# Delta-rule stage of a hybrid block: pairs of chunks overlapped on alternating banks, outputs alternating halves

## The reference, cut to what matters

```python
def gdn_chunked(q, k, v, log_a, beta, s0):
    ...
    g = jnp.cumsum(log_a.reshape(B, H, n, C), axis=-1)
    decay = jnp.where(incl, jnp.exp(jnp.where(incl, diff, 0.0)), 0.0)
    kb = k * beta
    a_mat = jnp.where(strict, jnp.einsum('bhnid,bhnjd->bhnij', kb, k) * decay, 0.0) + jnp.eye(C)
    rhs = jnp.concatenate([v * beta, kb * jnp.exp(g)[..., None]], axis=-1)
    sol = lax.linalg.triangular_solve(a_mat, rhs, left_side=True, lower=True)
    u, w = sol[..., :DV], sol[..., DV:]
    qk = jnp.einsum('bhnid,bhnjd->bhnij', q, k) * decay
    ...
    def step(s, xs):
        v_new = u_c - w_c @ s                 # einsums, per head
        o = qd_c @ s + qk_c @ v_new
        s = s * ge_c + ke_c.T @ v_new
```

## Time and profile before

| | |
|---|---|
| profiled execution | 2245.06 us, span 2243.3 us, mean granted clock 0.935 |
| TensorE busy | 2012.8 us (90%) |
| VectorE busy | 1165.2 us (52%) |
| ScalarE busy | 992.2 us (44%) |
| GpSimd busy | 141.7 us (6%) |
| DMA | 254.61 MB, mean 114 GB/s |
| the delta-rule stage | from 1066.11 (first sums) to 1302.98 (last output copy) |

### The profile page before, as it was taken

How to read it: one execution, slowest core, us unless ns; L and a number is a source line. 1 busy time by engine, 2 the same in 40 slices (tenths; PEclk the granted TensorE clock), 3 DMA queues, 4 the chain that set the end, 5 groups by cost and what they waited for, 6 DMA issues and landing times.

```text
span 2243.3 us, 41597 instructions
## 1 busy us (share of the span) xinstructions
PE 2012.8 (90%) x16886; PEld 1763.1 (79%) x16886; DVE 1165.2 (52%) x1785; ACT 992.2 (44%) x1590; POOL 141.7 (6%) x132
## 2 busy tenths in 40 slices
PE   5998899979999999899788879998778998798997
PEld 4783687867878778688677869997677998677997
DVE  4421678734533442554455447645556655676654
ACT  5333477523431332445322246544745545455543
POOL 0000100001000001000323210010010000010000
PEclk8999899859999999999899979999989999999999
DMA  8330377512233323333100035663334665404663
GB/s 265 87 118 19 112 209 238 157 38 75 85 94 94 94 87 93 86 85 113 31 4 4 2 89 159 182 185 112 103 104 135 185 177 169 113 21 140 185 179 115
DMA packets 441804, 254.61 MB, mean 114 GB/s; under 512 B 10816, under 2 KB 440512, under 8 KB 441536
## 3 DMA queue, kind: packets, MB, share of 16 engines
q1 hardware_dynamic: 441664, 252.59, 38.9%
HBM read 251.51 MB, written 1.05 MB: 113 GB/s over the span
## 4 chain that ended last, share of the span: by engine, by line
PE 81%; DVE 10%; ACT 5%; issue 2%; DMA 1%; POOL 0%; DVEq 0%; ACTq 0%; SPq 0%; POOLq 0%
PE bank L378 20%; PE bank L380 19%; PE bank L379 19%; PE bank L370 3%; PE bank L603 2%; PE bank L604 2%; PE bank L1876 2%; DVE weights_lo L328 2%; ACT weights_hi L321 2%; PE bank L941 1%; PE bank L1168 1%; PE bank L1978 1%; PE bank L611 1%; PE bank L1892 1%; PE bank L475 1%
## 5 line engine op out<-in xcount | busy, mean ns | idle before, releaser
L328 DVE TENSOR_TENSOR weights_lo<-ring,weights_hi 128x1024 fp32r<-128x1024 f32 x472 | 578.2, 1230 | 471.4 <-ACT weights_hi L321 467.6
L378 PE MATMUL bank<-x_hi,weights_hi 128*128 128x256 f32 (+1 forms) x2024 | 644.1, 318 | 82.4 <-DVE x_lo L406 29.4
L321 ACT ACTIVATE weights_hi<-ring 128x1024 fp32r<-128x1024 f32 x472 | 495.1, 1054 | 352.4 <-PE bank L380 317.7
L380 PE MATMUL bank<-x_hi,weights_lo 128*128 128x256 f32 (+1 forms) x2024 | 636.8, 315 | 0.0
L379 PE MATMUL bank<-x_lo,weights_hi 128*128 128x256 f32 (+1 forms) x2024 | 636.7, 315 | 0.0
L378 PEld LDWEIGHTS bank<-x_hi,weights_hi 128*128 128x128 f32 x2024 | 389.5, 192 | 115.0 <-issue 87.8
L379 PEld LDWEIGHTS bank<-x_lo,weights_hi 128*128 128x128 f32 x2024 | 389.0, 192 | 24.5 <-issue 1.2
L380 PEld LDWEIGHTS bank<-x_hi,weights_lo 128*128 128x128 f32 x2024 | 389.3, 192 | 23.9
L378 PE MATMUL bank<-hidden_hi,weights_hi 128*128 128x256 f32 (+1 forms) x864 | 270.7, 313 | 10.0 <-DVE hidden_lo L1442 6.8
L380 PE MATMUL bank<-hidden_hi,weights_lo 128*128 128x256 f32 (+1 forms) x864 | 271.9, 315 | 0.0
L379 PE MATMUL bank<-hidden_lo,weights_hi 128*128 128x256 f32 (+1 forms) x864 | 271.6, 314 | 0.0
(11 more groups left out here) (316 smaller groups left out, 2449.8 us busy)
## 6 DMA issues: line engine op xcount, KB each, us to landing
ring<-mlp_w SPq DMA_DIRECT2D x128, 512.0 KB, 4.0
ring<-ada_w SPq DMA_DIRECT2D x96, 512.0 KB, 4.7
ring<-w_ffn_in SPq DMA_DIRECT2D x88, 512.0 KB, 4.7
ring<-w_ffn_out SPq DMA_DIRECT2D x32, 512.0 KB, 3.7
ring<-gdn_w_in SPq DMA_DIRECT2D x24, 512.0 KB, 3.9
ring<-even_w_in SPq DMA_DIRECT2D x18, 512.0 KB, 4.9
ring<-w_out SPq DMA_DIRECT2D x16, 512.0 KB, 5.2
ring<-w_in_a SPq DMA_DIRECT2D x14, 512.0 KB, 3.8
```

What stands on the lines that cost most here:

```text
L321: nc.scalar.activation(w_hi[:, g % AHEAD, :], ring[:, g % RAW, :], ACT.Copy).then_inc(hi_done[g % AHEAD].sem, 1)
L328: nc.vector.tensor_tensor(w_lo[:, g % AHEAD, :], ring[:, g % RAW, :], w_hi[:, g % AHEAD, :].bitcast(F32), ALU.subtract).then_inc(lo_done[g ...
L378: pe.matmul(dst, lhs[0](k), rhs[0](k), start=start and k == 0, stop=False)
L380: last = pe.matmul(dst, lhs[1](k), rhs[0](k), start=False, stop=stop and k == nk - 1)
```

## The change

- Pairs use banks by turns: pair `p`, unit `z` has `bank[4z + 2(p % 2)]` and the next one for everything: levels, values, weights and steps. The separate `bank_r` is gone.
- `DE`, `NA`, `XT` and `XX` exist twice. The second set lies in the memory of `weights_lo`. So the low parts of the four first output tiles are no longer made in `dve_odd_in`, but one by one in the last part of the stage. For pair 3 the last state, decayed queries, `QKT` and `U` lie in memory of earlier buffers.
- The head of pair `p + 1` is taken apart and placed among the levels of pair `p` on every engine. The values of pair `p` come after the matrix start of `p + 1`; its weights stand in level 0 of `p + 1`.
- For the latent pairs, the query sums and query-key products stand in the levels of pair 3.
- The outputs of both latent pairs are accumulated in the same four banks, so VectorE copies each once. Products with the states alternate between the two halves of rows and so between two banks. They are placed between the steps of pair 3.
- The norm's first squares wait for the first two output copies instead of all. SyncE's load of the next tables waits for the same last copy, counted anew.

```diff
+        with nc.sbuf_tensor("spare", [P, AHEAD * TILE], F32) as spare:
+            pass
         w_lo = sb("weights_lo", [P, AHEAD, TILE], F32R)
...
+        DE1, NA1, XT1, XX1 = (by_heads(spare[:, i * UNIT:(i + 1) * UNIT], C) for i in range(4))
+        DE, NA, XT, XX = (DE0, DE1), (NA0, NA1), (XT0, XT1), (XX0, XX1)
...
             for i in range(VB):
-                split_lo(dve, odd_tiles.first + NB_CONV + i + AHEAD)
+                if i + AHEAD < VB:
+                    split_lo(dve, odd_tiles.first + NB_CONV + i + AHEAD)
...
-        def bank_a(z):
-            return bank[4 * z]
...
+        def bank_of(p, z, i):
+            return bank[4 * z + 2 * (p % 2) + i]
...
         def pe_gdn_ws(pe, p, st):
...
+                pe.wait_ge(N["wtc"], u + 1)
+                if st == 1 and p < 2:
+                    pe.wait_ge(N["d"], 2 * (p + 2) + z + 1)
+                if st == 1 and p == 2:
+                    pe.wait_ge(N["qe"], z + 1)
...
+        def obank(b):
+            return bank[(0, 1, 4, 5)[b]]
+        def pe_gdn_o_values(pe, p, h2):
+            pe.wait_ge(N["vn"], 4 * (p + 1))
+            pe.wait_ge(N["qkt"], 4)
+            for par in range(2):
+                b = 2 * h2 + par
+                for i in range(2):
+                    hd = 2 * (2 * h2 + i) + par
+                    for z in range(2):
+                        at = (2 * i + TBS[p][z]) * P
+                        ins = pe.matmul(obank(b)[:, at:at + P], U[p][:, z, hd, :], QKT[p][:, z, hd, :], ...)
+        def pe_gdn_o_states(pe, p, h2):
+            pe.wait_ge(N["ss"], 2 * p + 8)
+            pe.wait_ge(N["qd"], 2 * (p - 1))
+            for i in range(2):
+                hp = 2 * h2 + i
+                for z in range(2):
+                    for st in range(2):
+                        c = st if z == 0 else 1 - st
+                        at = (2 * i + TBS[p][z]) * P + c * C
+                        for par in range(2):
+                            pe.matmul(obank(2 * h2 + par)[:, at:at + C], state(2 * p + st, z, hp, half(par)),
+                                      qdcs[p][half(par), z, hp, c * C:(c + 1) * C], ...)
         def pe_gdn(pe):
...
+            for p in range(4):
+                pe_gdn_q(pe, p, 0)
+                if p >= 1:
+                    pe_gdn_weights(pe, p - 1)
+                pe_gdn_z(pe, p, 0)
+                for st in range(2):
+                    pe_gdn_q(pe, p, 1 + st)
+                    if p >= 1:
+                        pe_gdn_ws(pe, p - 1, st)
+                    pe_gdn_z(pe, p, 1 + st)
+                    if p >= 1:
+                        pe_gdn_su(pe, p - 1, st)
+                    if p == 3:
+                        pe_gdn_query_sums(pe, 2 + st)
+                    elif st == 0:
+                        pe_gdn_sums(pe, p + 1)
+                pe_gdn_q(pe, p, 3)
+                if p < 3:
+                    pe_gdn_keys(pe, p + 1)
+                else:
+                    pe_gdn_query_keys(pe, 2)
+                    pe_gdn_query_keys(pe, 3)
+                pe_gdn_z(pe, p, 3)
+                pe_gdn_q(pe, p, 4)
+                pe_gdn_z(pe, p, 4)
+                if p < 3:
+                    pe_gdn_first(pe, p + 1)
+                pe_gdn_values(pe, p)
+            pe_gdn_weights(pe, 3)
             pe_gdn_ws(pe, 3, 0)
+            pe_gdn_o_values(pe, 2, 0)
+            pe_gdn_o_states(pe, 2, 0)
             pe_gdn_su(pe, 3, 0)
+            pe_gdn_o_values(pe, 2, 1)
             pe_gdn_ws(pe, 3, 1)
-            pe_gdn_o(pe, 3)
+            pe_gdn_o_states(pe, 2, 1)
+            for h2 in range(2):
+                pe_gdn_o_states(pe, 3, h2)
+            for h2 in range(2):
+                pe_gdn_o_values(pe, 3, h2)
...
         def act_gdn(act):
+            act_gdn_eyes(act, 0)
+            act_gdn_decay(act, 0)
             for p in range(4):
+                if p >= 1:
+                    act_gdn_values(act, p - 1)
+                act_gdn_level(act, p, 0)
+                if p >= 1:
+                    act_gdn_weights(act, p - 1)
+                act_gdn_level(act, p, 1)
+                if p == 3:
+                    act_gdn_query(act, 2)
+                act_gdn_level(act, p, 2)
+                if p == 3:
+                    act_gdn_query(act, 3)
+                else:
+                    act_gdn_decay(act, p + 1)
+                act_gdn_level(act, p, 3)
+                if p < 3:
+                    act_gdn_eyes(act, p + 1)
+                act_gdn_level(act, p, 4)
...
         def dve_gdn(dve):
...
+            for p in range(4):
+                dve_gdn_level(dve, p, 0)
+                for st in range(2):
+                    if p >= 1:
+                        dve_gdn_vn(dve, p - 1, st)
+                    dve_gdn_level(dve, p, 1 + st)
+                    if p >= 1:
+                        dve_gdn_ss(dve, p - 1, st)
+                    if p < 3 and st == 0:
+                        dve_gdn_decays(dve, p + 1)
+                dve_gdn_level(dve, p, 3)
+                if p < 3:
+                    dve_gdn_below(dve, p + 1)
+                else:
+                    dve_gdn_query(dve, 2)
+                dve_gdn_level(dve, p, 4)
+                if p < 3:
+                    dve_gdn_first(dve, p + 1)
+            dve_gdn_query(dve, 3)
             dve_gdn_vn(dve, 3, 0)
+            out_tiles = odd_tiles.first + NB_CONV + VB
+            dve.wait_ge(N["wt"], 8)
+            split_lo(dve, out_tiles)
             dve_gdn_ss(dve, 3, 0)
+            split_lo(dve, out_tiles + 1)
             dve_gdn_vn(dve, 3, 1)
+            split_lo(dve, out_tiles + 2)
+            for b in range(4):
+                dve_gdn_out(dve, b)
+            split_lo(dve, out_tiles + 3)
...
         def pool_gdn(pool):
...
+            for p in range(4):
+                if p >= 1:
+                    pool_gdn_scale_keys(pool, p - 1)
+                    pool_gdn_sg(pool, p - 1, 1)
+                if p < 3:
+                    pool_gdn_below(pool, p + 1)
+                if p == 2:
+                    pool_gdn_query_masks(pool, 2)
+                if p == 3:
+                    pool.wait_ge(N["wt"], 6)
+                    nc.gpsimd.memset(QKT[3], 0.0).then_inc(N["clear"], 1)
+                    pool_gdn_query_masks(pool, 3)
+                    pool_gdn_scale_queries(pool, 2)
+                if p < 2:
+                    pool_gdn_masks(pool, p + 2)
+                if p >= 1:
+                    pool_gdn_sg(pool, p, 0)
+            pool_gdn_scale_queries(pool, 3)
+            pool_gdn_scale_keys(pool, 3)
...
         def act_odd_out(act):
-            act.wait_ge(N["oc"], 8)
             for i in range(4):
+                act.wait_ge(N["oc"], 2 * (i // 2) + 2)
                 nc.scalar.activation(as_heads(obuf(osq, i)), two_heads(i), ACT.Square).then_inc(OT["squares"], 1)
```

More of the change, by code:

```diff
@@ L1497, in state @@
         def state(i, z, hp, rows=slice(0, P)):
+            if i == 7:
+                return last_state[rows, z, hp, :]
             if i % 3 == 0:
@@ L1908, in pe_gdn_tail @@
                     for c in range(2):
-                        ins = pe.matmul(four((bank_a(z), bank_b(z))[c])[half(hd % 2), hd // 2, :],
-                                        ktk[half(c), TBS[p][z], hd * C:(hd + 1) * C], XX[half(c), z, hd, :], start=True, stop=True)
+                        ins = pe.matmul(four(bank_of(p, z, c))[half(hd % 2), hd // 2, :],
+                                        ktk[half(c), TBS[p][z], hd * C:(hd + 1) * C], XX[p % 2][half(c), z, hd, :],
+                                        start=True, stop=True)
@@ L1930, in pe_gdn_ws, with pe_gdn_query_sums @@
+        def pe_gdn_query_sums(pe, p):
+            for z, u in units(p):
+                for hd in range(NH):
+                    col = la[:, TBS[p][z], z * NH + hd:z * NH + hd + 1].broadcast_to((P, C))
+                    ins = pe.matmul(bank_of(2, z, 1)[half(hd % 2), (hd // 2) * P:(hd // 2 + 1) * P], col, upto[:, z, :],
+                                    start=True, stop=True)
+                ins.then_inc(N["g2"], 1)
         def pe_gdn_ws(pe, p, st):
@@ L1969, in pe_gdn_o @@
                     for z in range(2):
-                        pe.matmul(o[:, (2 * i + z) * P:(2 * i + z + 1) * P], U[:, z, hd, :], QKT[:, z, hd, :],
-                                  start=i == 0 and z == 0, stop=False, skip_group_check=True)
-                for i in range(2):
-                    hp = 2 * h2 + i
-                    for z in range(2):
-                        for st in range(2):
-                            c = st if z == 0 else 1 - st
-                            at = (2 * i + z) * P + c * C
-                            ins = pe.matmul(o[:, at:at + C], state(2 * p + st, z, hp, half(par)),
-                                            qdc[half(par), z, hp, c * C:(c + 1) * C], start=False,
-                                            stop=i == 1 and z == 1 and st == 1, skip_group_check=True)
@@ new lines, in pe_gdn_o_values @@
```

(11 more changed lines are left out.)

309 lines of the change are left out of this document (125 added, 184 removed).

## The result

The changed kernel takes 2191.42 us (median of four runs, 2189.05 to 2191.99). The kernel before took 2239.28 us beside it (2239.13 to 2245.18), and the ratio is 0.977 with a 95% interval of 0.975 to 0.979. So 47.9 us went. The forecast was 47.6 us, to 2191.6. One execution of a later kernel, the one with eight unused products, took 3271.61 us at a mean granted clock of 0.551; it stands in none of the medians here.

The account below looks back on a forecast made before the run. TensorE was taken as the bound, 81% of the chain of waits. Gains of 32.2 (pairs), 13.1 (tail) and 3.5 (norm), less 1.2, gave 47.6 us: from the 2239.18 median to 2191.6, range 2177 to 2215.

Parts of the forecast that it names:

- fourth pair: Last pair of the delta-rule stage: output products leave, query work enters; 36.4 us work plus 5.0 gaps, 41.4 for 45.4.
- tail: After the fourth pair's values, to the last output copy: covered steps and state products at 0.12 us, 24.9 for 38.0.
- norm: Norm after the outputs: half the squares start 1.4 us sooner, four sums at full clock save 2.1; gain 3.5 us.
- moved splits: Four low parts of weights moved into the stage's tail, 1.23 us each on VectorE; one charged, 1.2 us lost.
- The heads: Serial sums, keys and inversion start before each pair: waits, 3.29 us and earlier engines' steps, fall beside TensorE work.
- The pauses: First pair's levels: 5.2 us of "issue", TensorE waiting for nothing the profile shows; no reordering removes it, so it stays.
- rival (a): TensorE's issue pauses vanish as slower pieces between levels let issue catch up: up to 18.2 us more, 2173; 7%.
- Rival (b): VectorE's fixed order becomes the bound, copies queue behind subtraction and head work: three pairs lose 5 us each, 2207; 20%.
- rival (c): Half clock stays in the tail: output matmuls take up to twice as long, norm's sums 2.1 us more, 2207; 13%.
- Rival (d): Alternating row halves in the tail's state products overlaps nothing: 7.7 us more, 2199; 10%.
- Rival (e): Slower: half clock spreads from the tail backward through the second to fourth pair, costing 108 us, 2300; 3%.
- Marks: Signs expected in the changed profile: level 0 start times, values' end, last copy, TensorE gaps, tail clock, and wrong-if limits.

## Why the prediction was right

The steps, in the two profiled executions:

| step | forecast gain | measured |
|---|---|---|
| first pair, 43.8 to 34.6 | 9.2 | 10.8 (33.0) |
| second pair, 45.6 to 39.2 | 6.4 | 7.6 (38.0) |
| third pair, 53.2 to 40.6 | 12.6 | 14.0 (39.2) |
| fourth pair, 45.4 to 41.4 | 4.0 | 1.6 (43.8) |
| tail, 38.0 to 24.9 | 13.1 | 15.1 (22.9) |
| norm | 3.5 | 3.7 |
| moved splits | -1.2 | not seen |
| sum | 47.6 | 52.8 |

The sum of the traces is 5 us more than that of the medians, 47.9. The profiled execution of before was 5.8 us above its median, and the stage of after was at the short end of its scatter. So the table as a whole is a little large, though which terms of it is not known, and the agreement of the totals to 0.3 us is partly luck: two executions of one kernel differ by 2.3 us in the stage alone, and the terms miss by up to 2.4 us each.

**The heads.** The mechanism was right. What my working lacked is that the head also costs the clock. I took TensorE's work and the wait and let the windows' clock of 0.94 pass into the start's 3.0 us; the run with serial heads shows 22.5 us for three of them, 13.6 of idle time and 8.9 of slower products. The sum came out right as I took TensorE's work at full clock and set it against windows of before that had the half clock in them.

**The pauses.** 5.2 us of "issue" in the first pair were kept in the forecast, and rival (a) gave them up. They stayed: in the chain of waits over the fourth pair they are still 13.1%.

```profile
by line: PE bank L1900 16.7%; issue 13.1%; PE bank L1917 11.0%; PE bank L1926 9.1%; PE bank L1957 8.7%; PE bank L1914 8.3%; DVE a L2184 7.4%; PE bank L1986 7.3%; PE bank L1974 6.3%; PE bank L1949 4.9%; PE bank L1936 2.3%; DVE spare L2166 1.
```

**The fourth pair** is the term that was off. I forecast 5.0 us of gaps, with the work at 36.4; busy time is 36.5, and the gaps are 7.3. 13.1% of 43.8 us are 5.7 us of pauses, which I had not counted here as such, and 7.4% is VectorE's query multiplication ahead of the copies, 3.2 us of the chain:

```profile
1222.92 3.48 DVE L2184 TENSOR_TENSOR a<-bank,arena 64x256 f32<-64x256 f32 x8
1226.43 0.72 DVE L2166 COPY_PREDICATED spare<-tables,bank 128x512 f32<-128x512 int32 x1
```

I had named this place and given it, with the empty cover behind level 4, 1.0 us. The values' wait is 2.26. Rival (b), VectorE's order as the bound, is true at this one place and nowhere else: it costs 2 us, not 15.

**The tail.** 0.12 us for a state product was taken between 0.09 and 0.24; it is 0.11. The 8.7 us for value products are 7.9 (2.05, 2.05 and 3.84). The clock was the open point. I gave rival (c) 13% and argued against it with TensorE's waiting ahead of the output products, and with the same products at the whole clock at 1248. Both facts hold, but neither settles the tail: without the alternation the clock fell with TensorE busy without a break. My forecast of 1.00 had no working for what the order of the halves does to the clock, and in that it was luck; it held since the change also alternates them. Had the alternation been left out, the stage would have been 14 us longer, near the 15.1 of (c), though half of it is the products themselves.

**Rival (d)**, alternation overlaps nothing, is out by the 0.11. **Rival (e)** is out: every window shows 1.00, and in the executions where the clock did fall within the pairs it came back.

**Marks.** Level 0 of pairs two to four was forecast near 1112, 1151 and 1192, and stands at 1110.4, 1148.4 and 1187.6; values end at 1231.4 for 1233, the last copy at 1254.3 for 1258. "No gap over 1.5 us" does not quite hold: TensorE pauses 1.64 us at 1220.92, inside a level's second half, and waits 2.26 us for the values. "Wrong if a pair takes over 44 us" was a near thing: the fourth took 43.8 in this execution and 45.3 in the second profile of the same kernel. TensorE does not stand idle for a weight tile ahead of the output projection: its wait there is 8.05 us for VectorE's `x_lo`, and was 8.06 before.

**How the 50 us of the stage divide.** Put back one at a time in the kernel after, serial heads cost 23.8 us, one-sided products 12.7 at their own place (14.2 over the stage), outputs behind the steps 2.5 (6.0). These are 39 to 44 of 50. Each is measured from the 186.9 us; from the second profile's 189.2 each stage figure is 2.3 less. The rest was not isolated; the whole-bank output copies and the moved query work are in it.

## What to carry to other kernels

Where TensorE is the bound and each block of work begins with a chain over four engines, put the next block's head into this block's body: it gave back the wait (13.6 us here) and also the half-clock stretch behind it (8.9). Where products use 64 rows of the weights, let the upper and lower half take turns, with a bank each; here it halved the time of each product and kept the clock, and the changed loops alone gave 0.8% of the whole program. Once few gaps are left, look for pauses at a fixed number of records: here they went with the instruction's number and not with what stood there. Fewer instructions would be the thing to try; no run tried it.

## What the runs showed of the hardware that was not expected

- Full activity does not keep the clock. In three executions of two kernels it was at 0.52, 0.54 and 0.67 over stretches of 21 to 22 us with TensorE busy 93 to 100% of them, where state products (64 rows, 128 columns) came from one half of the rows at a time; with the halves alternating it held 1.00 with TensorE busy 8.7 of 12 us. It is not a rule of one-sided products alone, which also ran 12.1 us at 1.00. The cause was not isolated further: whether the row halves, the banks or the rate of products decides was not tried apart.
- In dense 64x64 products TensorE pauses 0.4 to 1.9 us at many of the steps of 254 to 256 records, which are 3.3 to 4.0 us apart there. The place follows the instruction's number.
- 60 waits on semaphores became 30 instructions.
